# Two FFN output stages: Strassen's scheme for the first pair of column chunks too, and the late hidden chunks spread over 28 units

## The reference

```python
def swiglu(x, w_in, w_out):
    gate, up = jnp.split(x @ w_in, 2, axis=-1)
    return (jax.nn.silu(gate) * up) @ w_out          # w_in 2048 x 11264, w_out 5632 x 2048

h = x + 0.5 * swiglu(rmsnorm(h), ffn1_w_in, ffn1_w_out)
...                                                  # mixer and cross attention
h = h + 0.5 * swiglu(rmsnorm(h), ffn2_w_in, ffn2_w_out)
out = rmsnorm(h, final_norm)
```

## Time and profile before

| | us |
|---|---|
| median of 3 runs | 2098.63 |
| lowest, highest | 2097.04, 2099.12 |
| the profiled execution, its own time | 2096.39 |
| its span, first to last instruction | 2094.4 |

### The profile page before, as it was taken

How to read it: one execution, slowest core, us unless ns; L and a number is a source line. 1 busy time by engine, 2 the same in 40 slices (tenths; PEclk the granted TensorE clock), 3 DMA queues, 4 the chain that set the end, 5 groups by cost and what they waited for, 6 DMA issues and landing times.

```text
span 2094.4 us, 26439 instructions
## 1 busy us (share of the span) xinstructions
PE 2085.7 (100%) x9357; PEld 1732.6 (83%) x9357; DVE 1649.3 (79%) x1843; ACT 1133.5 (54%) x1301; POOL 38.3 (2%) x50
## 2 busy tenths in 40 slices
PE   9999999999999999999999999999999999999998
PEld 8888888888888888888888888888888888888887
DVE  8999998986888676566665666569999899977786
ACT  7555555554555565456544555455555555545554
POOL 0000000000000040000000000000000000000000
PEclk9999999999999999999999999999999999999999
DMA  8777666688676867875587776676666666697664
GB/s 300 224 232 238 215 213 222 211 256 271 207 228 222 281 227 215 252 209 184 174 290 240 233 212 188 188 252 208 227 220 230 223 209 213 216 321 218 194 202 161
DMA packets 185328, 472.50 MB, mean 226 GB/s; under 512 B 17056, under 2 KB 67616, under 8 KB 185120
## 3 DMA queue, kind: packets, MB, share of 16 engines
q1 hardware_dynamic: 183088, 464.11, 70.0%
q0 software_dynamic: 1728, 6.82, 1.0%
q10 hardware_dynamic: 432, 0.53, 0.1%
HBM read 443.60 MB, written 27.79 MB: 225 GB/s over the span
## 4 chain that ended last, share of the span: by engine, by line
PE 99%; issue 0%; ACT 0%; DVE 0%; ACTq 0%; POOLq 0%; DVEq 0%; POOL 0%
PE acc L2099 15%; PE acc L2101 15%; PE acc L2102 15%; PE acc L2123 11%; PE acc L2122 11%; PE acc L2124 11%; PE acc L2207 3%; PE acc L2205 3%; PE acc L2206 3%; PE aux L2122 1%; PE aux L2124 1%; PE aux L2123 1%; PE tp L2123 1%; PE tp L2124 1%; PE tp L2122 1%; PE acc L2315 1%
## 5 line engine op out<-in xcount | busy, mean ns | idle before, releaser
L802 ACT ACTIVATE w_hi<-raw 128x1024 fp32r<-128x1024 f32 x765 | 801.3, 1058 | 776.6 <-PE acc L2102 362.2
L1304 DVE TENSOR_TENSOR w_lo<-raw,w_hi 128x1024 fp32r<-128x1024 f32 x765 | 925.7, 1223 | 336.0 <-ACT w_hi L802 332.6
L2099 PE MATMUL acc<-w_hi,a_hi 128*128 128x512 f32 x680 | 264.8, 389 | 0.0
L2101 PE MATMUL acc<-w_lo,a_hi 128*128 128x512 f32 x680 | 264.6, 389 | 0.0
L2102 PE MATMUL acc<-w_hi,a_lo 128*128 128x512 f32 x680 | 264.6, 389 | 0.0
L2099 PE MATMUL acc<-w_hi,b_hi 128*128 128x512 f32 x512 | 200.4, 391 | 0.0
L2101 PE MATMUL acc<-w_lo,b_hi 128*128 128x512 f32 x512 | 199.3, 389 | 0.0
L2102 PE MATMUL acc<-w_hi,b_lo 128*128 128x512 f32 x512 | 199.3, 389 | 0.0
L2122 PE MATMUL acc<-w_hi,a_hi 128*128 128x512 f32 x460 | 178.9, 389 | 0.0
L2123 PE MATMUL acc<-w_lo,a_hi 128*128 128x512 f32 x460 | 178.9, 389 | 0.0
L2124 PE MATMUL acc<-w_hi,a_lo 128*128 128x512 f32 x460 | 178.9, 389 | 0.0
(11 more groups left out here) (360 smaller groups left out, 3198.6 us busy)
## 6 DMA issues: line engine op xcount, KB each, us to landing
raw<-in_ffn_w_in SPq DMA_DIRECT2D x349, 512.0 KB, 4.3
raw<-in_ffn_w_out SPq DMA_DIRECT2D x176, 512.0 KB, 4.2
raw<-in_w_mix_in SPq DMA_DIRECT2D x80, 512.0 KB, 4.4
raw<-in_w_ckv SPq DMA_DIRECT2D x64, 512.0 KB, 4.4
memq<-bounce SPq DMA_DIRECT2D x196, 128.0 KB, 4.2
bounce<-stage SPq DMA_DIRECT2D x37, 512.0 KB, 5.3
raw<-in_w_mix_out SPq DMA_DIRECT2D x32, 512.0 KB, 4.5
raw<-in_w_cq SPq DMA_DIRECT2D x32, 512.0 KB, 4.2
```

The costliest lines, as they stand in the source:

```text
L802: eng.activation(w_hi[:, u % RING], raw[:, u % RING], ACT.Copy).then_inc(w_hi_done, 1)
L1304: eng.tensor_tensor(w_lo[:, u % RING], raw[:, u % RING], w_hi[:, u % RING].bitcast(f32), ALU.subtract).then_inc(w_lo_done, 1)
L2099: eng.matmul(dst, x_hi[:, rows], w_hi[:, slot, i], start=start and i == 0, stop=False)
L2101: eng.matmul(dst, x_hi[:, rows], w_lo[:, slot, i], start=False, stop=False)
```

## The change

- Chunks 0 and 1 become a pair of 44 units, with four groups (inner tiles 0 to 7) among 36 plain units. The order is: 12 plain units (left and right of inner units 4 to 9), then four times a group and two plain units (groups at positions p = 12, 16, 20, 24), then plain units, left and right in turn, at the end four left and four right.
- The second pair keeps its order of 8 groups. The mixes of the first four groups serve both pairs. They are made at p = 2, 4, 6, 8 of the first pair, the other four at p = 28, 30, 32, 34.
- The late hidden chunks are turned at p = 0, 4, 8, 16, 20, 24, 28, and each one's `fetch` stands on SP's queue at the same p, ahead of load p. From the fourth on they are turned into `stage` (the banks of `tp` hold sums by then), after the last hidden chunk was sent.
- The reload of x (or h) moves from units 4 to 7 to p = 12, 16, 20, 24.
- The first pair ends as the second does: ACT copies P1 at p = 37, DVE adds P6 and P7 at 38, forms the left sums and takes off P5 at 42, then a left residual, and at p = 0 and 2 of the second pair the two halves of the right one. PE starts the second pair once the left sums are read.
- h1's first chunk (FFN 1) is sent from h at p = 4 of the second pair, fetched at 8, turned at 10; its second chunk is sent at 10, fetched at 14, turned at 22 as before.

The host lays the same number of units out in the new order. The diff, cut to the order, SP's loop, DVE's loop and PE's loop:

```diff
-LATE_TURN_AT = [3 * i for i in range(FJ - DC)]
-LATE_FETCH_AT = [0] + [at + 5 for at in LATE_TURN_AT[:-1]]
+LATE_TURN_AT = [0, 4, 8, 16, 20, 24, 28]
+LATE_FETCH_AT = LATE_TURN_AT
+LATE_IN_TP = 3
...
-OUT_FAST = 8
-OUT_LEAD = 4
-def out_order():
-    plain = [(0, u) for u in range(OUT_FAST, U22)] + [(1, u) for u in range(OUT_FAST, U22)]
-    order, plain = plain[:OUT_LEAD], plain[OUT_LEAD:]
-    for s in range(OUT_FAST):
+OUT_GROUPS = (4, 8)
+OUT_MIXES = OUT_GROUPS[1]
+def out_order(q):
+    fast = OUT_GROUPS[q]
+    if q == 0:
+        lead, last = 12, U22 - 4
+        plain = [(side, u) for side in range(2) for u in range(fast, U8)]
+        plain += [(side, u) for side in range(2) for u in range(U8, U8 + 2)]
+        plain += [(side, u) for u in range(U8 + 2, last) for side in range(2)]
+        plain += [(side, u) for side in range(2) for u in range(last, U22)]
+    else:
+        lead = 4
+        plain = [(side, u) for side in range(2) for u in range(fast, U22)]
+    order, plain = plain[:lead], plain[lead:]
+    for s in range(fast):
         order += [("fast", s), ("fast", s)] + plain[:2]
         plain = plain[2:]
     return order + plain
...
+OUT_MIX_AT = [2, 4, 6, 8, 28, 30, 32, 34]
+H_AGAIN_AT = [12, 16, 20, 24]
+OUT_SUMS_AT = (38, OUT_FAST_END[1] + 3)
+OUT_LEFT_AT = (42, OUT_FAST_END[1] + 4)
+OUT_SEND_AT = [4, OUT_FAST_AT[1][1] + 2]
+OUT_FETCH_AT = [8, OUT_FAST_AT[1][2] + 2]
+OUT_TURN_AT = [OUT_FAST_AT[1][1] + 2, OUT_FAST_AT[1][4] + 2]
...
-                for u in range(U22):
-                    if u == RING:
+                for p in range(OUT_PAIR):
+                    if p == H_AGAIN_AT[0]:
                         eng.wait_ge(w_used, fast_done(in_base))
-                    if RING <= u < RING + DC:
-                        h_again(in_base, u - RING)
-                    if u == U8:
+                    if p in H_AGAIN_AT:
+                        h_again(in_base, H_AGAIN_AT.index(p))
+                    if p == U8:
                         send(number(TURNS, hid, FJ - 1), stage[:], hid_done, silus[in_base] + FJ)
-                    if u in LATE_FETCH_AT:
-                        fetch(number(TURNS, hid, LATE_CHUNKS[LATE_FETCH_AT.index(u)]))
-                    load(w, u, base, u)
-                for u in range(U22):
-                    if name is not None and u == U8:
-                        send(number(TURNS, name), stage[:], res_done, number(RESIDUAL, name) + 1)
-                    if name is not None and u == U8 + 2:
-                        fetch(number(TURNS, name))
-                    load(w, U22 + u, base, U22 + u)
+                    if p in LATE_FETCH_AT:
+                        fetch(number(TURNS, hid, LATE_CHUNKS[LATE_FETCH_AT.index(p)]))
+                    load(w, p, base, p)
                 for p in range(OUT_PAIR):
-                    if name is not None and p == OUT_SEND_AT:
-                        send(number(TURNS, name, 1), stage[:], res_done, number(RESIDUAL, name, 1) + 1)
-                    if name is not None and p == OUT_FETCH_AT:
-                        fetch(number(TURNS, name, 1))
-                    load(w, 2 * U22 + p, base + 2 * U22, p)
+                    if name is not None and p in OUT_SEND_AT:
+                        send(*from_h(name, OUT_SEND_AT.index(p)))
+                    if name is not None and p in OUT_FETCH_AT:
+                        fetch(number(TURNS, name, OUT_FETCH_AT.index(p)))
+                    load(w, OUT_PAIR + p, base + OUT_PAIR, p)
...
+                    if p in LATE_TURN_AT:
+                        i = LATE_TURN_AT.index(p)
+                        c = LATE_CHUNKS[i]
+                        if p == 0:
+                            eng.wait_ge(gate_read, FJ * (1 + TURNED.index(hid)))
+                        if i < LATE_IN_TP:
+                            turn_fill(hid, c, number(TURNS, hid, c))
+                        else:
+                            eng.wait_ge(sent, 16 * number(TURNS, hid, FJ - 1) + 16)
+                            eng.wait_ge(t_read, number(FILLS, hid, c))
+                            turn(number(TURNS, hid, c), stage4)
+                    if p - 1 in LATE_TURN_AT:
+                        i = LATE_TURN_AT.index(p - 1)
+                        c = LATE_CHUNKS[i]
+                        fill_lo(split_number(hid, c), hid_lo[:, 4 * c - KT:4 * c - KT + 4],
+                                hid_hi[:, 4 * c - KT:4 * c - KT + 4], src=tp[:] if i < LATE_IN_TP else stage4)
+                    if p - 2 in OUT_MIX_AT:
+                        weight_mixes_lo(OUT_MIX_AT.index(p - 2))
+                    if p in OUT_MIX_AT:
+                        if p == OUT_MIX_AT[0] and turn_no:
+                            eng.wait_ge(out_right_added, 2 * turn_no)
+                        mix_parts(OUT_MIX_AT.index(p), *x_parts, scratch=out_scratch, ready=out_mix_ready)
+                    if p == OUT_SUMS_AT[0]:
+                        sums_drained(0)
+                    if p == OUT_LEFT_AT[0]:
+                        eng.wait_ge(t_read, number(FILLS, hid, FJ - 1) + 1)
+                        left_summed(0)
...
+                left_residual(0, stage[:] if hi is None else chunk(0))
+                for p in range(OUT_PAIR):
+                    unit_lo(1, p)
+                    if p == 0:
+                        if hi is None:
+                            scaled_back(0)
+                        right_added(0, 1)
+                    if p == 2:
+                        eng.wait_ge(w_used, base + OUT_PAIR)
+                        eng.wait_ge(out_right_added, right_sums_done(0))
+                        if hi is None:
+                            eng.wait_ge(sq_done, number(SQUARES, name) + 1)
+                        eng.scalar_tensor_tensor(out=stage[:] if hi is None else chunk(1), in0=acc[:, NT:2 * NT],
+                                                 scalar=0.5, in1=chunk(1), op0=ALU.mult, op1=ALU.add
+                                                 ).then_inc(res_done, 1)
...
-                eng.wait_ge(res_done, number(RESIDUAL, name, 0) + 1)
-                for p in range(OUT_PAIR - (RING if name == "out" else 0)):
-                    if p in OUT_FAST_AT:
-                        fast(OUT_FAST_AT.index(p))
-                    elif OUT_ORDER[p][0] != "fast":
-                        plain(p)
+                eng.wait_ge(gate_read, silus[in_base] + FJ)
+                eng.wait_ge(t_read, number(FILLS, hid, DC - 1) + 1)
+                for q in range(2):
+                    if q:
+                        eng.wait_ge(out_left_summed, 2 * out_turn[hid] + 1)
+                    for p in range(OUT_PAIR - (RING if q and name == "out" else 0)):
+                        if p in OUT_FAST_AT[q]:
+                            fast(q, OUT_FAST_AT[q].index(p))
+                        elif OUT_ORDER[q][p][0] != "fast":
+                            plain(q, p)
```

More of the change, by code:

```diff
@@ L967, in ffn_out @@
-                    if p == OUT_FAST_AT[0] + 2:
-                        eng.wait_ge(res_done, number(RESIDUAL, name) + 2)
[L970 to L978, removed]
+                    unit_hi(1, p)
@@ new lines, in ffn_out @@
+                    if p == 1:
+                        eng.wait_ge(res_done, number(RESIDUAL, name) + 1)
+                        squares(name, 0, stage[:] if h_hi is None else h[:, :, 0:CH])
+                    if p == OUT_FAST_AT[1][0] + 2:
+                        eng.wait_ge(res_done, number(RESIDUAL, name) + 2)
+                        squares(name, 1, stage[:] if h_hi is None else h[:, :, CH:2 * CH])
+                    if p - 1 in OUT_TURN_AT and h_hi is not None:
+                        n = OUT_TURN_AT.index(p - 1)
+                        if n:
+                            eng.wait_ge(out_t_used, out_count(hid, 1, 2))
+                        fill_hi(turned, number(TURNS, name, n) + 1, h_hi[:, 4 * n:4 * n + 4], gain + 4 * n,
+                                src=stage4)
@@ new lines, in scaled_back @@
+                def scaled_back(n):
+                    eng.wait_ge(res_done, number(RESIDUAL, name, n) + 1)
+                    if hi is not None:
+                        eng.tensor_scalar(chunk(n), stage[:], 1.0, None, ALU.mult)
+                    for t in range(NT if hi is None else 0):
+                        eng.tensor_tensor(chunk(n)[:, t:t + 1], stage[:, t:t + 1],
+                                          final_gain[:, :, CH * n:CH * n + CH], ALU.mult)
+                for p in range(OUT_PAIR):
+                    unit_lo(0, p)
+                    if p == 2:
+                        hidden[0](FJ - 1)
+                    if p == 3:
+                        hidden[1](FJ - 1, 0)
+                        hidden[1](FJ - 1, 1)
+                    if p in LATE_TURN_AT:
[9 more added lines that the diff above has]
+                            turn(number(TURNS, hid, c), stage4)
+                    if p - 1 in LATE_TURN_AT:
+                        i = LATE_TURN_AT.index(p - 1)
```

(45 more changed lines are left out.)

289 lines of the change are left out of this document (134 added, 155 removed).

## The result

The changed kernel takes 2107.35 us (median of 6 runs, 2104.57 to 2109.33); the kernel before, beside it, 2097.84 us (2096.86 to 2100.55, 6 runs). The ratio is 1.0044 with a 95% interval of 1.0033 to 1.0054: slower by 9.5 us. The profiled execution took 2106.83 us.

What follows compares the result with a forecast made beforehand. TensorE was taken to bound the kernel, 99% of the chain. Per stage, stalls of 5.6 us less 2.72 removed gave +2.9, twice +5.8 on 2098.63: 2104.4 us; range 2095.5 to 2115, the forecast's own 2101 to 2109.

Steps and rivals of the forecast that it cites:

- First 12 units: Plain units before the first group: DVE's added work fits beside PE, no stall, lead of 0.8 us left at p = 12.
- Rival two: Everything is covered by DVE's lead, over 4 us at p = 12; the whole 5.44 us shows, 2093.2 us; chance 0.15.
- The round through SP: Rounds 16 to 20 and 20 to 24: turn, fetch, loads, sums, next turn take 12.6 us, 2.4 over PE's 10.2 each.
- The first late turn: Turn at p = 16, between two w_lo of a group: takes 1.17 us from a 0.8 us lead, 0.4 us lost.
- rival three: Transfers crowd the group rounds: landing 7.0 us, round 14.3 us, stalls 10 us per stage, 2113.5 us; chance 0.11.
- (e): The h reloads leave the crowded start and go to p = 12 to 24; costed at nothing.
- The tail: After the groups: the fetch at 28 delays plain units only, mixes leave DVE little to catch up; 0.4 us lost.
- (a): The first pair's drains, about 6.2 us instead of about 3, lie at p = 38 and later; costed at nothing.
- (b): One more residual before the second pair's first group: DVE needs 9.2 us, PE 13.6; costed at nothing.
- (c): h1's second turn and fill meet a round with 1.3 us to spare and some 4 us of lead; costed at nothing.
- (d): ScalarE is busy 5 to 6 of 10 us throughout; costed at nothing.
- (f): Turn 2's 2.93 us wait for its fetch goes; PE never waited for it, so nothing is gained.

Runs made afterwards that it cites:

- e3: Changed kernel with four plain units between the first pair's groups instead of two, turns, fetches and second four mixes moved to suit: 2093.93 us, ratio to before 0.9981.
- e1: Changed kernel with the fetches of the last three late chunks two units later, behind the group's two loads: 2103.7 us, ratio to before 1.0028.
- e2: Changed kernel with the late turns from the fourth on two units earlier, in plain units, and the fetch at p = 16 moved to 14: 2102.62 us.
- e5: Changed kernel with four fetches issued in plain units and the h reload behind the group rounds, turns left in the groups: 2097.57 us, ratio to before 0.9996.
- e4: Changed kernel with only the four h reloads moved, to p = 30 to 36 behind the group rounds: 2104.6 us, ratio to before 1.0029.
- e6: Changed kernel with late turns and fetches at p = 14, 18, 22, 26 and the h reload at p = 31 to 37: 2098.79 us, ratio to before 1.0003.

## Why the prediction was right in sign and short in size

Forecast 2104.4 us, measured 2107.35, within the forecast's own range of 2101 to 2109 and slower, as predicted. The rise was larger than the two times suggest: the sum gave +5.8 us, and the median rose by 9.5. The forecast stood on 2098.63, and the kernel before measured 2097.84 beside the change; that 0.8 us made the miss look smaller, which was luck. Point by point:

- **Removed, 5.44 us.** Right; 9333 matmuls, and e3, which has no loss in the output stages, lies 4.5 us under the kernel before (interval 2.1 to 5.9 us).
- **First 12 units, no stall, a lead of 0.8 us at p = 12.** Right. DVE was busy 30.97 of 32.7 us there and PE lost nothing; the w_lo of unit 12 ended near 497.5, about 1.3 us before PE wanted it at 498.77. Rival two needed a lead of over 4 us and falls.
- **The round through SP, 12.6 us.** Right, link by link: 0.1 + 1.85 + 0.49 + 5.39 + 0.08 + 2.66 + 1.14 + 1.24 (the turn itself) = 12.95 us in the first, 12.2 in the second with a landing of 4.68. PE lost 2.7 and 1.8 us in these two, 2.5 and 3.2 in the second FFN: 2.5 on average, forecast 2.4. e1, e2 and e5 show that it was this chain, by taking it off in steps: 12.2 to 13.5 us in the change, 11.2 to 12.6 with the fetch moved (e1), 11.2 to 12.5 with the turns moved (e2), 11.1 to 11.2 with the queue cleared (e5). PE's waits name w_lo in the groups, as predicted; the low parts of the sums are late as well, but only the spacing shows it.
- **The first late turn, 0.4 us.** This term was mis-sized: PE lost 1.9 us in the group at p = 16 (1.4 in the second FFN). The sum let the first round, 12 to 16, run at DVE's 8.9 us and kept the lead for the turn. But the group's second load could go only at 498.65, when the w_lo of p = 13 had freed its slot (it ended at 498.62), and the reload at p = 12 and the fetch at p = 16 stood ahead of it, so it landed after 6.44 us. DVE idled 2.61 us, and the lead was spent before the turn came. So this round closed through the ring of four slots, a chain that the prediction did not price and that e1 uncovered in the later rounds. The prediction had that 7 us landing in rival three and put it into the later rounds, and under (e) it costed the moved reload at nothing. The later rounds' landings were 4.7 to 5.6 us with the reload and 4.7 to 5.5 without it, and e4 left those rounds at 12.2 to 13.05 us: rival three falls for them, and its mechanism is true of the first.
- **The tail, 0.4 us (the fetch at 28).** Nothing was lost there.
- So 6.7 and 7.3 us per stage, the small excesses included, stand against 5.6: 2.8 us of the 4.7 by which the span's rise of 10.5 us exceeds the 5.8. Another 1.5 us lie in FFN 1's input product, where PE waited for t_lo_part (L1469). All of this is counted beyond what the kernel before loses there. With the same code in that product, e5 lost 1.5 us too, e2 0.7, and e1, e3, e4 and e6 nothing. It varies from execution to execution; no step of the change is known to cause it, and its cause stays open.
- **Costed at nothing:** (a), (b) and (c) hold, as PE lost nothing in the second pair; (d) as well, ScalarE is at 24.37 of 48 us in the stretch. (f) does too: no turn waits for its fetch in the change. (e) does not hold, as said.
- **The Trainium skill's fit** ("DMA: Bandwidth & Descriptors", anatomy of one DMA) would have given, as an estimate, 3.2 us for a load. The page of the profile has 4.3 as the median. In the change, the second load of the first group took 3.4 us (issued at 489.65, with nothing else of SP's queue on its way), and those of the groups with a late turn took 4.7 to 6.4. With the queue cleared the rounds did come out as by that rule, DVE's load alone binding (e5), but through landings of 4.3 to 5.0 us, not through 3.2.

## What to carry to other kernels

Before side work is put beside a shortened stretch of the bounding engine, add up for one round the other engine's whole work, and every chain that closes through a buffer: the one through the single fetch buffer and, behind it, the one through the ring of weight slots. Here DVE's own work made 11.1 to 11.2 us, the chain through the fetch buffer 12.2 to 13.5 and the one through the slots 11.2 to 12.6 (e1), against PE's 10.2, and removing the longest only uncovered the next. What brought a gain was to lengthen the round: the same groups with two more plain units between them, and the turns among those units (e3), covered all three. PE lost nothing there, and the median fell by 4.5 of the 5.44 us.

## What the runs showed of the hardware beyond what was expected

- How long a load of 512 KB took on this queue depended on what was on its way with it. The second load of the group at p = 16 took 4.3 and 4.5 us (first and second FFN) with only loads about it (e5), 5.5 and 5.4 us behind a fetch of the same size in small pieces (e4), 6.4 and 5.9 us behind a fetch and a reload (the change): 0.5 to 1.15 us for each half megabyte ahead.
- That is no rule for a forecast. In e3 a load with only loads ahead took 6.2 us, with a reload and a fetch issued behind it. The second loads of the groups at p = 20 and 24 took 4.0 to 6.0 us in e1, with a fetch issued 0.43 us behind them, and 4.4 to 5.0 in e5, with one 0.43 to 0.77 us behind. What makes them differ was not tried.
- A matmul that had waited is drawn 0.50 us long instead of 0.39, and the next one starts 0.34 us after it instead of 0.23. At the waits with brackets of 0.21, 0.61 and 0.97 us the spacing lost 0.48, 0.88 and 1.24: each of these waits cost 0.27 us more than its bracket. Of that, 0.16 us is the part of the matmul before that is drawn beyond its spacing (0.39 less 0.23), and 0.11 us the later start of the next. So the view of waits had 7.1 us for w_lo where the spacing had 13.4, and none where the spacing had 3.7. Whether the matmul itself takes longer or is only drawn so was not tried.
